# Mixer buffers laid over a 21-slot weight ring, so that the expert weights of the next stage are requested while a mixer still runs

## What is computed

```python
for layer in range(2):
    u = rms_norm(h, norm_mix[layer])
    if layer == 0:   # hybrid: RWKV-7 heads beside sparse attention heads
        mix = concat([rwkv7_mix(...), nsa_mix(...)]) @ hyb_w_out
    else:            # Mamba-2
        mix = mamba2_mix(u, ssm_w_in, ..., ssm_w_out)
    h = h + mix
    h = h + hier_moe(rms_norm(h, norm_ffn[layer]), ...)
return rms_norm(h, norm_final)
```

## Time and profile before

| | us |
|---|---|
| median of the three runs shown (1542.73 to 1549.9) | 1544.51 |
| the profiled execution, its own time | 1538.09 |
| its span, first to last instruction | 1536.3 |
| `hyb` begins, `experts` of layer 0 begins | 0, 264.8 |
| first gate/up product, last expert's output copied, layer 0 | 287.7, 753.95 |
| `ssm` begins, `experts` of layer 1 begins | 765.65, 1024.4 |
| first gate/up product, last expert's output copied, layer 1 | 1048.8, 1515.4 |

### The profile page before, as it was taken

How to read it: one execution, slowest core, us unless ns; L and a number is a source line. 1 busy time by engine, 2 the same in 40 slices (tenths; PEclk the granted TensorE clock), 3 DMA queues, 4 the chain that set the end, 5 groups by cost and what they waited for, 6 DMA issues and landing times. The chain is left out here.

```text
span 1536.3 us, 22145 instructions
## 1 busy us (share of the span) xinstructions
PE 1403.4 (91%) x8946; PEld 780.2 (51%) x8946; DVE 418.7 (27%) x1025; ACT 278.1 (18%) x538; POOL 10.0 (1%) x12
## 2 busy tenths in 40 slices
PE   7999998899999999888699998988999999998884
PEld 3778884444444444333288886544444444443331
DVE  0148744311111121211135735223111111221112
ACT  2242322110101001000133553111010101000001
POOL 0000000000000000000000010000000000000000
PEclk9999979899999999999899998998999999999997
DMA  9410110999999999999463440149999999999992
GB/s 288 155 55 19 40 57 26 423 420 422 420 422 421 421 422 420 421 421 420 190 240 118 145 176 1 65 166 420 421 421 421 422 422 421 421 420 422 421 420 120
DMA packets 85453, 459.69 MB, mean 299 GB/s; under 512 B 10704, under 2 KB 16080, under 8 KB 36080
## 3 DMA queue, kind: packets, MB, share of 16 engines
q1 hardware_dynamic: 85360, 458.38, 73.8%
HBM read 457.30 MB, written 1.05 MB: 298 GB/s over the span
## 5 line engine op out<-in xcount | busy, mean ns | idle before, releaser
L1778 PE MATMUL bank<-rawffn,xgffn 128*64 128x512 f32 x1152 | 255.6, 596 | 0.0
L1722 DVE TENSOR_TENSOR aTffn<-bank,sgffn 128x256 f32<-128x256 f32 (+1 forms) x64 | 23.5, 367 | 638.4 <-ACT sgffn L1661 638.4
L1793 PE MATMUL bank<-rawffn,xgffn 128*32 128x512 f32 x896 | 147.5, 647 | 42.3 <-DMA rawffn<-in_moe_w_up 22.2
L1778 PEld LDWEIGHTS bank<-rawffn,xgffn 128*64 128x64 f32 x1152 | 81.4, 138 | 157.6 <-issue 155.7
L2342 PE MATMUL bank<-uT,wr 128*128 128x256 f32 x640 | 143.5, 384 | 0.0
L1747 PEld LDWEIGHTS bank<-selffn,uxffn 128*128 128x128 f32 x1024 | 125.8, 200 | 28.7 <-issue 26.8
L1816 PE MATMUL bank<-rawffn,aTffn 128*64 128x512 f32 x576 | 131.5, 598 | 9.1 <-DVE aTffn L1722 9.1
L1747 PE MATMUL bank<-selffn,uxffn 128*128 128x128 f32 (+1 forms) x1024 | 134.3, 287 | 3.3 <-DVE hitsffn L1554 2.0
L1658 ACT COPY gusffn<-bank 128x512 f32<-128x512 f32 x64 | 37.5, 585 | 532.3 <-PE bank L1778 316.9
L2342 PEld LDWEIGHTS bank<-uT,wr 128*128 128x128 f32 x640 | 121.7, 192 | 18.1 <-issue 1.9
L1840 PE MATMUL bank<-ysffn,selTffn 64*128 64x512 f32 x512 | 127.2, 615 | 1.7 <-DVE ysffn L1734 1.7
(11 more groups left out here) (360 smaller groups left out, 1237.4 us busy)
## 6 DMA issues: line engine op xcount, KB each, us to landing
rawffn<-in_moe_w_gate SPq DMA_DIRECT2D x128, 1024.0 KB, 24.4
rawffn<-in_moe_w_up SPq DMA_DIRECT2D x128, 1024.0 KB, 26.0
rawffn<-in_moe_w_down SPq DMA_DIRECT2D x128, 1024.0 KB, 25.7
wr<-in_ssm_w_in SPq DMA_DIRECT2D x10, 2048.0 KB, 8.7
wr<-in_hyb_w_in SPq DMA_DIRECT2D x5, 2048.0 KB, 8.0
wo<-in_ssm_w_out SPq DMA_DIRECT2D x4, 2048.0 KB, 10.9
gain<-in_rows SPq DMA_DIRECT2D x5, 512.0 KB, 12.9
wr<-in_hyb_w_in SPq DMA_DIRECT2D x1, 1760.0 KB, 14.1
```

Of the source, the lines that this page charges most:

```text
L1778: i = T.matmul(bank[GU_BANK][CAP * m:CAP * m + CAP, :], xg[:, odd, k, :], raw[:, slot, (k % 4) * FH:(k % 4 + 1) * FH], start=(k == 0), sto ...
L1793: i = T.matmul(bank[GU_BANK][CAP_S * c:CAP_S * c + CAP_S, :], xg_s[:, odd, 4 * half + k, :], raw[:, CHUNKS * ph + c, k * FH:(k + 1) * FH], ...
```

## The change

1. The ring becomes one array `raw` of 21 slots of 1 MiB, allocated for the whole program at the bottom of the free memory. The mixers' buffers lie over the same addresses, in an order in which the ones that are done with first come first. The routers' scratch (`hg`, `uT`, `junk`) lies over the last two slots.
2. `load_ahead` issues the first chunks of the next expert stage from inside the mixer's block. In `hyb`: slots 0 to 5 after `out 7`, 6 to 11 after the last `qs`, 12 to 16 after `turnr 1`: 17 chunks. In `ssm`: 0 to 4 after the last projection group, before the third load of `wo2`; 5 to 8 behind that load; 9 to 12 behind the fourth; 13 and 14 after the last gating: 15 chunks. The block itself then loads up to slot 18, and 19 and 20 once the logits exist.
3. The ring goes round by chunks, not by experts: chunk n lies in slot n % 21 and waits for chunk n - 21.
4. `BIG` goes from 18 to 10, `FIXED` from 3 to 4. The 11th in the order and all after it have 32 places each. Each expert's own capacity (`caps`) is kept, and if any count is over it, the overflow pass runs, now over 20 experts (`OVER`), with two experts' worth of slots. DVE works that out behind the sort.
5. `experts`, `overflow` and `close` are one block. All 16 pairs are written out, without the loop.
6. In layer 0 SP issues `wdt`, `mpar` and the first three groups of `ssm_w_in` behind the last chunk, after expert 29's gate/up products.
7. The table with Sqrt is loaded at the end of the expert block on ACT, no longer in `norm_act`.

```diff
-RING = 3
-FIXED = RING
-BIG = 18
-OVER = 12
+NSLOT = 21
+FIXED = -(-NSLOT // CHUNKS)
+BIG = 10
+OVER = FIXED + 16
+OVER_RING = 2
@@ norm_act
-        warm_table(act, ACT.Sqrt)
@@ the ring, and what is loaded ahead
+    raw = ring_area("raw", [P, NSLOT, DC])
+    hg_, uT_ = (Area(AREA + (NSLOT - 2 + i) * SLOT_BYTES) for i in range(2))
+    def load_ahead(sp, layer, first, last):
+        for n in range(first, last):
+            load_chunk(sp, layer, n // CHUNKS, n % CHUNKS, n, raw_main[n])
@@ hyb, sync
             for k in range(4):
                 load(sp, "wj", wo_r[k], wv_hyb[:, k, :])
+            sp.wait_ge(*at("out", 7))
+            load_ahead(sp, 0, 0, hyb_attended)
+            sp.wait_ge(*at("qs", 1, 1))
+            load_ahead(sp, 0, hyb_attended, hyb_carried)
+            sp.wait_ge(*at("turnr", 1))
+            load_ahead(sp, 0, hyb_carried, hyb_half)
@@ router_sync
-            for e in range(FIXED):
-                for c in range(CHUNKS):
-                    load_chunk(sp, main_pass, e, e, c)
+            load_ahead(sp, layer, ahead[layer], NSLOT - 2)
             load_gain(sp, NORMS[2 * layer + 2])
+            sp.wait_ge(*at("uhi", tag, 1))
+            sp.wait_ge(*at("logits", tag))
+            load_ahead(sp, layer, NSLOT - 2, NSLOT)
@@ main_sync
+            for n in range(NSLOT, NCHUNK):
+                s, c = divmod(n, CHUNKS)
...
+                was, piece = divmod(n - NSLOT, CHUNKS)
+                sp.wait_ge(ps.s["used"], USES * (b0 + was) + FREED[piece])
+                load_chunk(sp, layer, e, c, n % NSLOT, raw_main[n % NSLOT])
@@ sort
+                    if r == BIG // 8:
+                        did(V.tensor_scalar(caps[:, :], key[:, 0, :], high[:, BIG % 8:BIG % 8 + 1], float(CAP_S - CAP),
+                                            ALU.is_le, ALU.mult))
...
+                did(V.tensor_scalar(caps[:, :], caps[:, :], float(CAP), None, ALU.add))
+                did(V.tensor_tensor(count[:, :], count[:, :], caps[:, :], ALU.subtract))
+                did(V.tensor_reduce(over[:, 0:1], count[:, :], AX.X, ALU.max))
@@ the blocks
             def _(sp):
+                router_sync(sp)
+                main_sync(sp, main_pass, base)
+                then(sp, base)
+                sp.wait_ge(main_pass.s["tiles"], layer + 1)
                 more(sp, body)
@@
+                act_pass(act, main_pass, base, base2, MAIN_PLAN)
+                act.wait_ge(main_pass.s["tiles"], layer + 1)
                 more(act, body)
+                warm_table(act, ACT.Sqrt)
@@
+                pe_pass(pe, main_pass, base, base2, MAIN_PLAN, lambda s, c: main_piece(layer, s, c), True)
+                pe.wait_ge(main_pass.s["tiles"], layer + 1)
+                more(pe, body)
+                for part in range(4):
+                    nc.tensor.matmul(bank[ACC[part]][:, 0:1], C("ident"), C("before")[:, 0:1], start=False,
+                                     stop=True).then_inc(pe_done, PE.one(("close", tag, part)))
-        with nc.Block(name="close" + tag, no_gpsimd_drain=True) as block:
@@ the next mixer's weights, passed as then() for layer 0
+    def mixer_ahead(sp, b0):
+        sp.wait_ge(main_pass.s["used"], USES * (b0 + EXPERTS - 3) + 2)
+        load(sp, "small", wdt[:, :, :], w_ssm[:, :, DI + XBC:DI + XBC + MH])
...
+        for n in range(3):
+            load_group(sp, n)
@@ ssm, sync
             for g in range(GROUPS):
+                if g == 2:
+                    sp.wait_ge(*at("mgroup", len(MG) - 1))
+                    load_ahead(sp, 1, 0, 5)
                 if g >= 2:
                     sp.wait_ge(*at("joined", g - 2))
                 load(sp, ("wj", "par")[g % 2], wo2[:, g % 2, :, :], wv_ssm[:, 4 * g:4 * g + 4, :])
+                if g == 2:
+                    load_ahead(sp, 1, 5, mam_projected)
+                    sp.wait_ge(*at("ssmy", MH // 2 - 1))
+            load_ahead(sp, 1, mam_projected, mam_scanned)
+            sp.wait_ge(*at("gated", GROUPS - 1))
+            load_ahead(sp, 1, mam_scanned, mam_gated)
```

More of the change, by code:

```diff
@@ L299, in build @@
[L299 to L321, removed]
@@ new lines, in over_slot, with main_piece @@
+    def over_slot(s, c):
+        return OVER_SLOT + CHUNKS * (s % OVER_RING) + c
+    def main_piece(layer, s, c):
+        n = s * CHUNKS + c
+        slot = n % NSLOT
+        return slot, raw_main[slot], 16 * (layer * len(range(slot, NCHUNK, NSLOT)) + n // NSLOT + 1)
+    hyb = Area(AREA)
+    R4 = lambda name: hyb(name, [P, 4, SEQ])
+    nsac = hyb("nsac", [P, HALVES, 4 * HD])
+    zlo, lo3 = hyb("zlo", [P, 2, SEQ + 1]), hyb("lo3", [P, 2, SEQ])
+    par = hyb("par", [P, 4 * RW])
+    rn = hyb("rn", [HEADS, SEQ])
@@ new lines, in build @@
+    pc = hyb("pc", [P, 2, HALVES, 4, NCMP])
+    cmx = hyb("cmx", [P, 2 * HEADS])
+    nmx = hyb("nmx", [P, 8, GQ])
+    ss, std, rstd = (hyb(n, [P, HALVES]) for n in ("ss", "std", "rstd"))
+    kk = R4("kk")
+    pr = hyb("pr", [P, 2, GQ, SEQ])
+    pT = hyb("pT", [P, 2, 8, P])
+    nsav = hyb("nsav", [P, HALVES, 4 * HD + 24])
+    hyb_attended = hyb.slots()
+    front = hyb("front", [P, 4 * D])
+    z = hyb("z", [P, 12, SEQ + 1])
+    gts = hyb("gts", [P, HALVES, 24])
+    den = hyb("den", [P, 8, GQ])
@@ new lines, in build @@
+    otmp = hyb("otmp", [P, RW])
+    mixn = hyb("mixn", [P, HALVES, RW])
+    cum, exc, dd = R4("cum"), R4("exc"), R4("dd")
+    scl = hyb("scl", [P, 4, NCHK])
+    hyb_carried = hyb.slots()
+    kp = R4("kp")
+    zz = hyb("zz", [P, 12, SEQ])
+    gate = hyb("gate", [P, HALVES, RW])
+    uT = hyb("uT", [P, KD, SEQ])
+    qk = hyb("qk", [P, HALVES, 2 * HEADS, HD])
+    bon = hyb("bon", [P, HALVES, HEADS])
+    st8 = hyb("st8", [P, HALVES, HEADS])
+    hyb_half = hyb.slots()
+    mixr = hyb("mixr", [P, HALVES, RW])
@@ L1665, in run, with dve_pass @@
                     evict_x(1, "gb", "xb", t + 1, next_small)
-            every_pair(act, plan, looped, run)
-        def dve_pass(dve, ps, b0, p0, plan, looped, table, ids, sorts):
+            for t in range(len(plan)):
+                run(t)
+        def dve_pass(dve, ps, b0, p0, plan, table, ids, sorts):
             S = ps.s
@@ L1868, in run @@
                     pe.wait_ge(S["act"], b0 + e + 1)
-                    (down_s if small else down)(ph, landed)
+                    (down_s if small else down)(at_piece)
                     if odd and not last:
                         gather_b(t + 1, next_small)
-            every_pair(pe, plan, looped, run)
+            for t in range(len(plan)):
+                run(t)
             pe.wait_ge(S["y"], b0 + 2 * len(plan))
@@ L1910, in more @@
                     body(tau)
-        with nc.Block(name="overflow" + tag, no_gpsimd_drain=True) as block:
+        with nc.Block(name="experts" + tag, no_gpsimd_drain=True) as block:
             @block.sync
@@ L1986, in build @@
[L1986 to L1997 removed]
+            @block.tensor
@@ L2485, in _ @@
             joined(3)
-    mam.close()
-    experts(1)
+    experts(1, lambda sp, b0: None)
     with ExitStack() as fin:
```

383 lines of the change are left out of this document (180 added, 203 removed).

## The result

The changed kernel takes 1494.71 us (median of four runs, 1488.72 to 1499.24), beside 1543.62 us for the kernel before (1540.76 to 1549.90): a ratio of 0.9675, 95% interval 0.9625 to 0.9726, 48.9 us less. The profiled execution took 1498.02 us, span 1496.0. Against the profiled execution of before that is only 40.1 us less: the one was 5.5 us under its median, the other 3.3 us over. The comparison part by part is made between these two traces, and where the granted clock differs between them it says so.

A forecast was written before the change was run, and what follows sets the result against it. DMA's stream of expert weights was taken to set both stages' ends, with memory almost idle during the mixers. Terms -23.6 - 22.5 - 2 x 0.7 - 2 x 1.28 + 1 = -49.1 us, from 1544.5 to 1495.4; range 1484 to 1505, widened to 1512.

The forecast's parts named there:

- The forecast case: Whole kernel: the summed terms hold, -49.1 us, giving 1495.4 us; chance 0.74.
- The chunks ahead: Expert stages: chunks requested inside the mixers end the stream earlier, -23.6 us in layer 0 and -22.5 in layer 1.
- BIG = 10: Expert stages: ten large experts instead of 18 are worth 3 us a layer, already in the chunks' sum.
- The mixers are not disturbed: `hyb` and `ssm`: chunks queued ahead delay no mixer load; value 0, bounds 0 and +12.5 us.
- Rival B: `ssm`: mixer 1's output weights come late behind the chunks, up to 12.5 us, total 1508; chance 0.09.
- C: Expert stages: the ring does not fill early, only blocks and tables gain, about 1540 us; chance 0.04.
- D: After expert 31: the overflow pass runs, 308 us for each layer needing it, 1803 or more; chance 0.03.
- One block: End of each expert stage: two barriers go, -0.7 us a layer, some 4.8 us left for count load and branch.
- the branch under the weights: End of layer 0's stage: the branch may wait while mixer 1's weights stream, +1 us, bounds 0 and +5.5.
- the +3.2 of the bounds: Branch over the overflow pass: cost growing with ten pairs instead of six, +3.2 us a layer; 0 was taken.
- The table: Heads of `ssm` and `final`: no table load before the first Square, -1.28 us at each.
- Rival A: Small experts: PE at half clock throughout gives back 15 us a layer, total 1525; chance 0.08.

The follow-up runs named there:

- e1_no_ahead: The changed kernel without any chunk asked for inside a mixer, all 21 slots requested from the expert block itself; 1542.39 us, ratio 0.9989.
- e2: The changed kernel with BIG = 18 in place of 10; 1497.67 us, ratio 0.9706.
- e3: The changed kernel with mixer 1's first weights asked for at the start of `ssm`, not behind the last chunk; 1489.68 us, ratio 0.9642.
- e9_all: The changed kernel with BIG = 6, `close` ahead of PE's branch, and mixer 1's first weights asked for at the start of `ssm`; 1480.01 us, ratio 0.9592.
- u1_unrolled: The kernel before the change with its loops over pairs and SP's loop over experts written out, nothing else; 1540.02 us, ratio 0.9973.

## Why the prediction was right

The forecast case happened: 1494.7 where 1495.4 stood, and nearly the whole gain is the one it names. Its steps:

- **The chunks ahead, -23.6 and -22.5 us.** Measured -21.6 and -22.4; against e1_no_ahead, which has the same DMA rate, -23.8 and -24.2. Expert 9 ends 174.9 us after the norm (443.22 - 268.35); 174.7 was worked out. The first small expert's products end at 449.25, and chunk 189 is there at 726.50: less 2.6 us, 109 chunks in 274.7, 2.520 us each where 2.505 was taken. That 0.6% is the mis-sized term, 1.7 us in layer 0.
- **BIG = 10, 3 us a layer.** With 18 the wait comes 2.3 and 2.9 us later, counted from the first copy (e2).
- **The mixers are not disturbed.** The output weights' fourth load is asked for at 981.53 and no product of L2532 waits for DMA. Rival B did not come. Nor did C, since the ring stood full before the first slot came free (DMA moves nothing from 290 to 295.77), nor D, since `close` follows the last scatter.
- **One block, -0.7 us a layer, and the branch under the weights, +1.** This was the badly sized step. Layer 1 gained 3.6, layer 0 0.2. I had left 4.8 us for the load and the branch, unchanged: in fact both now begin while the last scatter is still being executed. Before, PE's load of the count begins at 757.18, 0.5 us after the scatter's end; now it begins at 738.11 and the branch at 739.00, and the scatter ends at 740.08. So the idle time falls from 5.73 to 2.28 us in layer 1 (the row of before stands below). That the branch now jumps over ten pairs instead of six costs nothing: it is recorded with 3.66 and 4.04 us before and 3.48 in layer 1 after, so the +3.2 of the bounds had no ground. In layer 0 the stream of mixer 1's weights takes 2.9 of it back (e3), about half of the 5.5 us that I had as its upper bound; the value of 1 was too low. Together -0.4 us was predicted and -3.8 measured. The range held both.

```profile
1523.86 1.84 PE L1960 MATMUL bank<-cst 128*128 128x1 f32 x8 [5.73 <-PEq L1912]
```

- **The table, -1.28 us twice.** From the final norm to the end: -1.4. ACT begins its Square at the head of both blocks with no table load ahead of it:

```profile
748.83 1.06 ACT L224 ACTIVATE front<-h 128x1024 f32<-128x1024 f32 x1 [11.47 <-PEq L1932]
...
1488.38 1.06 ACT L224 ACTIVATE junk_f<-h 128x1024 f32<-128x1024 f32 x1 [8.48 <-PEq L1932]
```

- **Rival A, half clock in the small phase.** The products of L1836 between 443 and 727 us:

```profile
L1836 PE MATMUL bank<-raw,xg 128*32 128x512 f32 x682 | 107.2, 619 | 30.8 <-DMA raw<-in_moe_w_up 16.6 <-DMA raw<-in_moe_w_gate 8.6 <-issue 5.6
```

A mean of 619 ns against the 900 that would have shown it, at a granted clock of 0.99 up to 720 us. In this stretch the products waited 19 times for a chunk, at most 1.5 us, and the weight loads 27 times, at most 2.4 us, and the level stayed at 2.4 GHz nearly everywhere. The Trainium skill ("TensorE: Matmul & The Clock Gate", HAM oscillation) describes a kernel with longer waits for DMA between groups of products, in which each wait threw the clock back. With the waits of this case the trace does not show that. At the very last wait the products did run slow (5.19 and 6.52 us for 26, against 3.62), which is the +1.6 and +1.4 in the tails; before had that in one layer, e9_all in none.
- **What was luck.** The two stages and the final block give -20.3 - 24.5 - 1.4 = -46.2 us, and the hidden table load at `ssm` another -1.3. That is 47.5 us, of which the clock had taken back 3.0 in the tails; and up to the first norm it took another 3.4. The streams gave 2.1 us less than predicted, the blocks' ends 3.4 more, and these errors offset each other. The 48.9 between the medians agrees with the predicted 49.1 better than the terms do.
- **Two slips in the working**, neither of which moves the forecast. The plateaus of the earlier trace rows are twelve slices each, at 420 to 423 GB/s. And the bounds of the branch give 1495.4 + 6.4 + 5.5 - 1 = 1506.3 as the forecast's upper end, not 1505.

## What to carry to other kernels

When a stream of loads sets the end of a stage and the stage before leaves the memory idle, start the stream there; each chunk asked for early is worth its own transfer time, but only until the buffer is full before its first slot comes free (here after some ten of 21 slots). After that look at the consumer: it must become faster than the stream as early as it can. And put a branch over rarely used code where its engine has nothing to hand over, with nothing else streaming: look at every engine of the block, since the second one's jump shows only when the first one's is gone.

## What was not expected of the hardware

- In the changed kernel and its variants a jump over the overflow pass stands for 2.2 to 2.8 us of idle time on PE behind the last scatter with no weights streaming, and for 5.2 to 5.3 us while they do; on DVE for at most 2.9 and 5.7 us. The difference is the start of the instruction packet, 0.9 to 1.3 us after the branch in the first case and 3.6 to 3.7 in the second, in every trace with the new ring.
- The same loads ran at 421 GB/s in the kernel before and in u1_unrolled, and at 419 in every trace of a kernel with the new ring, steadily. The cause is open.
- PE's work in `ssm`, 1176 recorded products each time, took 249.96 us in the changed kernel's trace and 245.46 in that of e9_all, at granted clocks of 0.96 and 0.98 (first fence the changed kernel, second e9_all):

```profile
749.00:1010.10 261.10, 249.96 (x1176) 187.75 (x1176) 112.80 (x246) 89.23 (x120) 9.84 (x8) 0.96 0.41 153
```

```profile
739.20:995.90 256.70, 245.46 (x1176) 183.67 (x1176) 112.92 (x248) 89.41 (x120) 9.84 (x8) 0.98 0.48 180
```

Such shifts of 4 us in one stretch are as large as most edits here. They go with the granted clock, so the clock of a stretch is to be read before its length is compared; and the size of an edit had to be read from its own stretch, not from the total.
